# Three narrow matmuls per weight tile for the outputs by channels, and one engine that evicts each of them in one step

## The reference

```python
proj = h @ w_in[l] + b_in[l]                # first block
u, lru_gate, q, k, v, mix_gates = jnp.split(proj, SPLITS, axis=-1)
...
proj = xn @ w_in[l]                         # second block
q = (_rmsnorm(c_q, q_norm_gain) @ w_uq).reshape(B, S, N_HEADS, dqk)
kv = (_rmsnorm(c_kv, kv_norm_gain) @ w_ukv).reshape(...)
...
gu = hn @ w_up[l]
g = _dwconv_centred(gu[..., :D_FF], ffn_conv_w[l], ffn_conv_b[l])
h = h + _rmsnorm((gelu(g) * gu[..., D_FF:]) @ w_down[l], post_ffn_gain[l])
```

## Time and profile before

| | |
|---|---|
| median of 3 runs | 2719.02 us |
| profiled execution, span | 2718.1 us |
| PE busy | 2692.5 us (99%), 13384 matmuls |
| PE's weight loads busy | 2267.3 us (83%), 13384 loads |
| DVE busy | 1892.7 us (70%), 2581 instructions |
| ACT busy | 1317.0 us (48%), 1874 instructions |
| DMA | 598.62 MB, 220 GB/s |

### The profile page before, as it was taken

The page is one execution under the profiler, slowest core; times in us unless marked ns, Lnnn a source line. Parts: engine busy times, 40 slices in busy tenths (PEclk is TensorE's granted clock), DMA queues, the critical chain, the costliest instruction groups (busy, mean ns, idle before and its releaser), DMA issues.

```text
span 2718.1 us, 34164 instructions
## 1 busy us (share of the span) xinstructions
PE 2692.5 (99%) x13384; PEld 2267.3 (83%) x13384; DVE 1892.7 (70%) x2581; ACT 1317.0 (48%) x1874; POOL 30.1 (1%) x60
## 2 busy tenths in 40 slices
PE   9999999999999999999999999999999999999998
PEld 6888888888887788888888888888888888888886
DVE  7878777888876665555554577778587657765775
ACT  4168675544444544344434456554464434543543
POOL 1100000000000000000000000000000000000000
PEclk9999999999999999999999999999999999999999
DMA  9964667899977686555555555544555555555553
GB/s 389 408 248 161 227 215 260 279 352 355 311 271 238 218 276 210 192 190 192 186 194 193 186 188 185 173 154 134 195 197 187 191 193 187 188 193 194 187 192 118
DMA packets 161833, 598.62 MB, mean 220 GB/s; under 512 B 18151, under 2 KB 18376, under 8 KB 160392
## 3 DMA queue, kind: packets, MB, share of 16 engines
q1 hardware_dynamic: 154824, 564.71, 61.2%
q0 software_dynamic: 6848, 31.72, 3.0%
HBM read 592.17 MB, written 4.19 MB: 219 GB/s over the span
## 4 chain that ended last, share of the span: by engine, by line
PE 94%; DMA 3%; DVE 2%; ACT 0%; issue 0%; SPq 0%; POOL 0%; DVEq 0%; ACTq 0%
PE PS L690 93%; DMA W<-in_ada_first 2%; DVE ACC L1999 1%; DMA G<-in_window 0%; PE PS L1126 0%; PE PS L921 0%; PE PS L1068 0%; DVE WL L1996 0%; DVE XBf L1996 0%; PE PS L1098 0%; PE PS L1222 0%; ACT WH L1347 0%; ACT TT L1670 0%; POOL out L679 0%; ACT XA L1669 0%
## 5 line engine op out<-in xcount | busy, mean ns | idle before, releaser
L1996 DVE TENSOR_TENSOR WL<-W,WH 128x1024 fp32r<-128x1024 f32 x876 | 1068.8, 1223 | 618.8 <-ACT WH L1347 617.3
L1347 ACT ACTIVATE WH<-W 128x1024 fp32r<-128x1024 f32 x876 | 924.1, 1058 | 804.9 <-PE PS L690 742.6
L690 PE MATMUL PS<-WH,XA 128*128 128x512 f32 (+1 forms) x2560 | 799.1, 390 | 4.3 <-DVE WL L1996 4.2
L690 PE MATMUL PS<-XA,WH 128*128 128x512 f32 x2480 | 798.6, 399 | 0.5 <-DVE XA L1999 0.5
L690 PE MATMUL PS<-WH,XB 128*128 128x512 f32 x1952 | 611.6, 391 | 0.0
L690 PEld LDWEIGHTS PS<-WH,XA 128*128 128x128 f32 x2560 | 480.5, 188 | 104.3 <-DVE WL L1996 3.1
L690 PEld LDWEIGHTS PS<-XA,WL 128*128 128x128 f32 x2480 | 466.2, 188 | 106.7 <-issue 0.7
L690 PE MATMUL PS<-WL,XA 128*128 128x512 f32 (+1 forms) x1280 | 496.6, 388 | 0.0
L690 PE MATMUL PS<-XA,WL 128*128 128x256 f32 x2480 | 491.7, 278 | 0.0
L690 PEld LDWEIGHTS PS<-WH,XB 128*128 128x128 f32 x1952 | 366.5, 188 | 75.8 <-issue 0.5
L690 PEld LDWEIGHTS PS<-XA,WH 128*128 128x128 f32 x2480 | 384.4, 189 | 2.7 <-DVE XA L1999 0.9
(11 more groups left out here) (233 smaller groups left out, 1376.5 us busy)
## 6 DMA issues: line engine op xcount, KB each, us to landing
W<-in_w_ffn_in SPq DMA_DIRECT2D x176, 512.0 KB, 3.7
W<-in_w_up SPq DMA_DIRECT2D x176, 512.0 KB, 3.8
W<-in_w_in SPq DMA_DIRECT2D x132, 512.0 KB, 4.1
W<-in_ada SPq DMA_DIRECT2D x128, 512.0 KB, 5.5
W<-in_w_ffn_out SPq DMA_DIRECT2D x88, 512.0 KB, 3.6
W<-in_w_down SPq DMA_DIRECT2D x88, 512.0 KB, 4.1
W<-in_ada_first SPq DMA_DIRECT2D x64, 512.0 KB, 9.3
W<-in_w_mix SPq DMA_DIRECT2D x64, 512.0 KB, 5.3
```

Source lines behind the costliest of these rows:

```text
L690: return e.matmul(o, l, r, start=start, stop=stop, skip_group_check=True)
L1347: return e.activation(o, a, ACT.Copy)
L1996: return e.tensor_tensor(o, a, b, op)
```

## The change

`pair` stays for the group of the second block alone. Everywhere else `gemm` calls the new `narrow`: three matmuls of 256 columns for each weight tile, `W_hi X_hi`, `W_hi X_lo` and `W_lo X_hi`, all three adding up in the same 256 columns of the bank. The order no longer alternates. The finished sum lies in the bank, and one engine evicts it in one step: ACT with the bias (u 14 and 15, kv, q), ACT with bias and gelu (gt), ACT's copy (kn, qn), or DVE with the multiplication by the inverse norm (h1, h2, x0, gg, gu).

```diff
+        def narrow(b, X, kt, whi, wlo, first, last):
+            o = b[:, 0:S]
+            mul(o, whi, X[kt][:, 0:S], first, False)
+            mul(o, whi, X[kt][:, S:2 * S], False, False)
+            return mul(o, wlo, X[kt][:, 0:S], False, last)
...
-                m = pair(bank_of(key), X, kt, whi, wlo, j == 0, last, j % 2 == 1)
+                m = narrow(bank_of(key), X, kt, whi, wlo, j == 0, last)
...
+        def biased(key, o, at, signal):
+            w.wait_ge(*mm[key])
+            e.activation(o, out_of_bank(key), ACT.Identity, bias=pv("b_in", at)).then_inc(*signal(key))
...
             units(("kv", o))
-            half(("kv", o), bias=pv("b_in", 48 + o))
+            biased(("kv", o), kT[:, o, :] if o < 4 else TEMP["v", o - 4], 48 + o, ea)
...
             units(("q", o))
-            half(("q", o), bias=pv("b_in", 32 + o))
+            w.wait_ge(*lrp[o])
+            biased(("q", o), QT[:, o, :], 32 + o, ea)
...
             units(("gt", o))
-            half(("gt", o), bias=pv("b_in", 16 + o))
             t = TEMP["gt", o]
-            w.wait_ge(*ev["gt", o])
-            e.activation(t, t, ACT.Gelu_apprx_tanh).then_inc(*fn(("gt", o)))
+            w.wait_ge(*mm["gt", o])
+            w.wait_ge(*(turned["v", o] if o < 4 else xl["yl", o - 4]))
+            e.activation(t, out_of_bank(("gt", o)), ACT.Gelu_apprx_tanh, bias=pv("b_in", 16 + o)).then_inc(*ea(("gt", o)))
...
         for h in range(8):
             units(("qn", h))
-            half(("qn", h))
+            w.wait_ge(*mm["qn", h])
+            copy(QN[:, h, :], out_of_bank(("qn", h))).then_inc(*ea(("qn", h)))
...
+        def times(key, o, by):
+            if key in IN_GROUP:
+                w.wait_ge(*eh[key])
+                tt(o, out_of_bank(key), half_of(key), ALU.add).then_inc(*ev(key))
+                w.wait_ge(*ev.last())
+                tt(o, o, by, ALU.mult).then_inc(*cv())
+                return
+            w.wait_ge(*mm[key])
+            tt(o, out_of_bank(key), by, ALU.mult).then_inc(*ev(key))
...
             w.wait_ge(*cv.last())
-            out_of(key, s[:, 1:1 + S])
+            times(key, s[:, 1:1 + S], by)
             w.wait_ge(*ev.last())
+            w.wait_ge(*cv.last())
             w.wait_ge(*sv.last())
-            if by is not None:
-                tt(s[:, 1:1 + S], s[:, 1:1 + S], by, ALU.mult).then_inc(*cv())
-                w.wait_ge(*cv.last())
```

More of the change, by code:

```diff
@@ L287, in banks_in_turn @@
             holder[i] = k, tb
-        if not is_moving(k):
+        if k in GROUPS[-1]:
             half[k], half_before[k] = m % 2, halves_of[m % 2]
@@ L588, in half_of, with out_of_bank @@
         return EV[HALF[key]]
+    def out_of_bank(key):
+        return bank_of(key)[:, 0:S]
     def chunk(n):
@@ L604, in freed @@
             return [(fn if key[0] == "fg" else el)["f", key[1], tb]]
-        return [(ea if key[0] in ("cq", "ck", "vn") else ev)[key]]
+        if key[0] == "u":
+            return [eu[key]]
+        return [(ea if key[0] in ("cq", "ck", "vn", "kv", "q", "gt", "kn", "qn") else ev)[key]]
     def sync(e):
@@ L1042, in v_turn @@
             w.wait_ge(*old)
-            w.wait_ge(*ev["kv", 4 + g])
+            w.wait_ge(*ea["kv", 4 + g])
             for tb in range(2):
@@ L1056, in head @@
             w.wait_ge(*old)
-            w.wait_ge(*ev["q", h])
-            w.wait_ge(*ev["kv", g])
+            w.wait_ge(*ea["q", h])
+            w.wait_ge(*ea["kv", g])
             mul(b[:, 0:P], QT[:, h, 0:P], kT[:, g, 0:P], True, True)
@@ L1203, in head2 @@
             w.wait_ge(*old)
-            w.wait_ge(*ev["qn", h])
-            w.wait_ge(*ev["kn", h])
+            w.wait_ge(*ea["qn", h])
+            w.wait_ge(*ea["kn", h])
             w.wait_ge(*cp["qp", h // 4])
@@ L1379, in group, with half @@
                     boundary(BEGIN[keys[0]][j // 2])
-        def half(key, bias=None, scale=None):
-            kw = {} if bias is None else {"bias": bias}
-            kw |= {} if scale is None else {"scale": scale}
+        def half(key):
             w.wait_ge(*mm[key])
@@ L1386, in half @@
                 w.wait_ge(*ev[HALF_BEFORE[key]])
-            e.activation(half_of(key), bank_of(key)[:, S:2 * S], ACT.Identity, **kw).then_inc(*eh(key))
+            e.activation(half_of(key), bank_of(key)[:, S:2 * S], ACT.Identity).then_inc(*eh(key))
+        def biased(key, o, at, signal):
+            w.wait_ge(*mm[key])
+            e.activation(o, out_of_bank(key), ACT.Identity, bias=pv("b_in", at)).then_inc(*signal(key))
         def square(name, i, acc, src, scale=None):
@@ L1555, in scalar @@
             units(("u", h))
-            half(("u", h), bias=pv("b_in", h))
+            w.wait_ge(*sv["up", h])
+            biased(("u", h), UP[h][:, 3:3 + S], h, eu)
         def v_turn(g):
@@ L1816, in scalar @@
         units(("h1", 0))
-        half(("h1", 0))
         row_of("t2", INV[:, :])
@@ L1820, in scalar @@
         units(("h2", 0))
-        half(("h2", 0))
         c_gained(0)
@@ L1824, in scalar @@
         units(("h1", 1))
-        half(("h1", 1))
         u_turn(0)
         units(("h2", 1))
-        half(("h2", 1))
         bg.width = 3
@@ L1833, in scalar @@
         for h in range(8):
-            half(("kn", h))
+            w.wait_ge(*mm["kn", h])
+            copy(KN[:, h, :], out_of_bank(("kn", h))).then_inc(*ea(("kn", h)))
             if h % 4 == 1:
@@ L1842, in scalar @@
             units(("h1", j))
-            half(("h1", j))
             if j == 2:
@@ L1851, in scalar @@
             units(("h2", j))
-            half(("h2", j))
         bg.drain()
@@ L1868, in scalar @@
             units(("x0", j))
-            half(("x0", j))
             if j == 0:
@@ L1890, in scalar @@
         attended(0, 1, 2, 3)
-        half(("x0", 7))
         boundary(BEGIN["x0", 7][1])
@@ L1956, in scalar @@
                 units(("gg", hh), part=slice(hh == 2, None))
-                half(("gg", hh))
+                if ("gg", hh) in IN_GROUP:
+                    half(("gg", hh))
                 units(("gu", hh), part=slice(0, 1))
@@ L1962, in scalar @@
                 units(("gu", hh), part=slice(1, None))
-                half(("gu", hh))
+                if ("gu", hh) in IN_GROUP:
+                    half(("gu", hh))
                 w.wait_ge(*mm[("gd", ci - 1, 3) if ci else ("mx", 3)])
@@ L2237, in conv4 @@
             s = UP[h]
-            w.wait_ge(*(eu if h < NU else ev)["u", h])
+            w.wait_ge(*eu["u", h])
             w.wait_ge(*sv["up", h])
@@ L2276, in vector @@
             units(("u", h))
-            w.wait_ge(*sv["up", h])
-            out_of(("u", h), UP[h][:, 3:3 + S])
         for o in range(8):
             units(("kv", o))
[L2282 to L2287, removed]
+            if o >= 4:
+                temps.take(("v", o - 4), turned, ("v", o - 4))
         def head(h):
@@ L2317, in vector @@
             units(("q", o))
-            w.wait_ge(*lrp[o])
-            out_of(("q", o), QT[:, o, :])
             bg.later(head(o))
@@ L2331, in vector @@
             units(("gt", o))
[L2332 to L2335, removed]
+            t, _ = temps.take(("gt", o), xl, ("yl", o))
+            w.wait_ge(*ea["gt", o])
             tt(t, t, Y[:, o, :], ALU.mult).then_inc(*el(("gt", o)))
@@ L2549, in conv_edges, with conv3 @@
                 e.memset(s[:, 257:258], 0.0).then_inc(*sv())
-        def conv3(key, ins, o, wname, bname, j, n, by=None):
+        def conv3(key, ins, o, wname, bname, j, n, by):
             s = ins[convs[0] % 3]
@@ L2646, in vector @@
         for h in range(8):
-            out_of(("kn", h), KN[:, h, :])
             if h % 4 == 1:
@@ L2651, in vector @@
             units(("qn", h))
-            out_of(("qn", h), QN[:, h, :])
         units(("qp", 0))
@@ L2841, in vector @@
                 w.wait_ge(*old)
-                out_of(("gu", hh), t2_)
+                times(("gu", hh), t2_, INV2)
                 w.wait_ge(*ev.last())
-                tt(t2_, t2_, INV2, ALU.mult).then_inc(*el())
-                w.wait_ge(*el.last())
+                w.wait_ge(*cv.last())
                 w.wait_ge(*fn["gg", hh])
```

## The result

| | before | after |
|---|---|---|
| median | 2719.59 us (2716.58 to 2722.73, 4 runs) | 2745.39 us (2744.87 to 2746.93, 4 runs) |
| profiled execution, span | 2718.1 us | 2743.4 us |
| PE matmuls | 13384 | 15832 |
| DVE busy | 1892.7 us | 1832.1 us |
| ACT busy | 1317.0 us | 1283.2 us |

The ratio is 1.0097, with a 95% interval of 1.0084 to 1.0110: slower, beyond the 0.2% that can be told from no change. The prediction had 2715 us, range 2703 to 2744. A fourth run of the kernel before (2722.73 us) has moved its median from 2719.02 to 2719.59.

What follows compares the result with a forecast made beforehand. PE's time from start to start was taken as the bound: 2448 tiles x 1.5 ns = 3.7 us off the 2718.1 us span gives 2714.4, plus 0.9 to the median 2715.3, rounded 2715 us; range 2703 to 2744.

Steps and rivals of the forecast that it cites:

- What bounds the kernel: Whole kernel: only PE's time from start to start counts, PE busy 99% of the span; ACT and DVE wait for it.
- The sum 2448 x (3c - 348.3 ns): PE, 2448 changed tiles: three narrow-matmul distances c replace 348.3 ns; even at c = 116.1 ns, 7.3 us per ns.
- c = 115.6 ns from the loads of the group: Narrow-to-narrow distance on PE, from 18 loads in 2.08 us where 128 and 256 columns alternate; 3.7 us gained.
- 114.8 ns for a narrow matmul: Distance read from narrow pairs between wide matmuls in PE's rows before the change; three would take 344.4 ns.
- The rival "each matmul has a fixed cost": On PE, the third matmul adds its own fixed cost: c = 120.0 ns, 28.7 us slower, 2748 us; chance 0.23.
- The far bound: On PE, the wide matmul's 20.3 ns surplus belongs to the high operand: 368.8 ns a tile, 50 us lost, 2769.
- ACT and DVE cost nothing; the new waits are covered: Some 48 us less ACT work and 70 us less DVE work count as nothing; ready weights, 11 us, cover ACT's waits.
- The rival of a new wait: A wait on ACT or DVE reaches PE; 0.5 us at each of 16 gt outputs makes 8 us, 2723; chance 0.05.
- the one of cheaper narrow matmuls: On PE, narrow matmuls really cost less, c = 113 to 114.8 ns: 9.5 to 23 us faster, 2696 to 2709; chance 0.15.

## Why the prediction was wrong

- **What bounds the kernel:** right. PE from start to start, and nothing else, set the time in every run; taking DVE's and ACT's work away changed the time by a ratio of 1.0000.
- **The sum 2448 x (3c - 348.3 ns), even at c = 116.1:** right in form. With the measured c = 120.0 it gives 28.6 us. The stretches by channels grew by 26.4, and the missing 2 us are in those where other products stand between the outputs, which the sum took to cost as much as the long ones. The spans differ by 25.3 since the token stretch gave 2.8 back with the clock and the front added 1.4, which the change does not touch either.
- **c = 115.6 ns from the loads of the group: the step that failed.** I took a stream of unequal matmuls for one limit by loads. A stream of equal ones has 111.6 ns at 128 and 192 columns and 120.0 at 256, where it is not the load that binds but the matmul's own 13.3 + 106.7 ns; 4.4 ns more in c, three times in each of 2448 tiles, are 32 us, and turn 3.7 us gained into 28.6 lost. The reading could not have been settled by the mean alone, but two numbers in the rows could have made me doubt it: the floor of 111.5 in the earlier trace rows, though of plain float32, and 120.0 from the earlier trace rows, whose mean is 115.8.
- **114.8 ns for a narrow matmul:** a true distance, but of two neighbours at a change of width. I allowed that part of its cost "could be hidden in the starts of the wide ones", and gave the rival 0.23. That the wide ones stood 7 ns too far apart, against 226.7 in the token rows, was the sign of it: the sum of the two was close to the rule (346.7) and the parts were not.
- **The rival "each matmul has a fixed cost"** had the mechanism, c = 120.0 and 2748 us; 2745.39 was measured. The page "TensorE: Matmul & The Clock Gate" of the Trainium skill, section "Back-to-back issue gap", gives the fixed part as about 2.5 ns, for the gap of a matmul taken by itself; in this kernel's product of rounded operands, each with its own load, it is 13.3, so the measurement decides. Its direction, against the third matmul, was right. I gave this rival 0.23 and still ended the range at 2744 us (c near 119.5), just under its own 120.0.
- **The far bound** (the surplus belongs to the high operand) fell: the distance behind high and low matmuls is the same 120.
- **ACT and DVE cost nothing; the new waits are covered:** right. ACT was 34 us and DVE 61 us less busy, less than the 48 and 70 I had counted; the counts of 124 and 166 instructions hold (1874 to 1750, 2581 to 2415). The term was mis-sized since I multiplied counts by recorded lengths, and instructions that follow at once overlap. The recorded lengths, added up over the trace, did fall by 47 us on ACT and 70 on DVE; the busy time counts an overlap once: before the change a copy of a half recorded with 0.37 us was followed by the next instruction 0.26 us after its start (the rows below). No wait for an eviction appeared on PE. The rival of a new wait fell, and so did the one of cheaper narrow matmuls.

ACT in time order, in the kernel before; start, length, instruction:

```profile
2004.87 0.37 ACT L1387 ACTIVATE EV<-PS 128x256 f32<-128x256 f32 x1
2005.13 1.05 ACT L1347 ACTIVATE WH<-W 128x1024 fp32r<-128x1024 f32 x1
```

## What to carry to other kernels

Where TensorE is busy throughout, count matmuls as well as columns: one product cut in two costs a fixed amount more, here 13.3 ns in 120 (some 2 ns for plain float32 in the same trace), and while those engines stay off the critical path no work saved on the engines that evict can pay for it. Take the cost of a matmul from a long stream of equal ones, or from a line through two widths; a distance beside a change of width, or a mean over two widths, belongs to neither. And ask of a limit whether it is one number: the longer of a floor and a matmul's own cost can look like a single value between them.

## What the runs showed of the hardware

- A matmul of these rounded float32 operands with its own weight load takes the longer of 111.6 ns and 13.3 ns + 0.4167 ns for each column, at widths of 128, 192, 256, 320, 384 and 512. At 320 and 512 columns it is the same with either operand standing still (146.7 and 226.7 ns); the other widths were run with the weights standing still.
- Behind narrow matmuls (256 columns) the next five wide ones (512) were 233, 236, 228, 232 and 231 ns apart instead of 227. In the long stretches wide and narrow by turns cost 353.3 ns a pair, two and two 348.3, eight and eight 349.2, sixteen and sixteen 347.9.
- The first narrow matmuls behind wide ones were 113 to 114 and 119 ns apart instead of 120. Whether they are really quicker, or only their recorded starts shift beside another width, the runs don't tell; the sums over both widths hold either way.
- Plain float32 with its own weight load: 215.8 ns at 256 columns, 430 at 512; with a single column 111 ns, about the floor above.
- Loading the same weights for the next matmul took as long as loading others: 120.0 ns in the orders high, high, low and high, low, high.
